# Zero matmuls on TensorE ahead of the transposes, the MLP loops and the router of a two-block transformer on one core

## The reference

```
# first block, two layers
x = x + rms(pool_mixer(rms(x)) )                      # layer 0 mixer
x = x + rms(relu(rms(x) @ w_up[0])**2 @ w_down[0])    # MLP, 4096 wide
k, v = split(rms(x) @ w_kv)
x = x + rms(stick_breaking_attention(rms(x) @ w_q, k, v) @ w_o)
x = x + rms(relu(rms(x) @ w_up[1])**2 @ w_down[1])    # MLP
# second block
proj = rms(x) @ w_in                                  # conv parts, q, k, v
h = x + concat(short_conv(proj), diff_attention(proj)) @ w_out
# hierarchical mixture: softmax over 4 groups, top 2 of 8 experts in the best group
comb = router(rms(h))                                 # 256 x 32 weights
out = h + sum_e comb[:, e] * (silu(rms(h) @ w_gate[e]) * (rms(h) @ w_up[e])) @ w_down[e]
```

## Time and profile before

| | before |
|---|---|
| median of 3 runs | 1189.21 us (1184.12, 1189.39, 1189.21) |
| the profiled execution's own time | 1188.13 us |
| its span, first to last instruction | 1186.2 us |
| PE busy | 957.2 us (81%), 5929 matmul records |
| PE weight loads | 715.6 us (60%) |
| DVE, ACT busy | 487.4 us (41%), 374.7 us (32%) |
| mean granted TensorE clock | 0.914 of full |
| DMA | 310.34 MB, mean 262 GB/s |

### The profile page before, as it was taken

One profiled execution on the slowest core, in us unless ns is written; L12 is line 12 of the kernel. 1 busy time (PEld: TensorE's weight loads), 2 busy tenths in 40 slices (PEclk: granted clock), 3 DMA queues, 4 the chain that ended last, 5 costly groups with the idle time before them and its releaser, 6 DMA issues.

```text
span 1186.2 us, 14708 instructions
## 1 busy us (share of the span) xinstructions
PE 957.2 (81%) x5929; PEld 715.6 (60%) x5929; DVE 487.4 (41%) x746; ACT 374.7 (32%) x633; POOL 1.9 (0%) x7
## 2 busy tenths in 40 slices
PE   5799999699778899999698887966666676666666
PEld 4799999599546899899588764431323142424232
DVE  3655655654545656556656674220202020201010
ACT  3545544554343545445454441100000000000000
POOL 0000000000000000000000000000000000000000
PEclk9899999899999899999899998996979787878889
DMA  9454554445103445545250477699999999999996
GB/s 361 185 212 155 199 212 150 150 145 211 71 1 142 151 152 212 192 161 212 72 179 35 181 292 307 281 431 429 429 433 430 430 431 431 433 431 431 429 427 248
DMA packets 62731, 310.34 MB, mean 262 GB/s; under 512 B 2529, under 2 KB 3553, under 8 KB 52321
## 3 DMA queue, kind: packets, MB, share of 16 engines
q1 hardware_dynamic: 62256, 308.17, 64.7%
q0 software_dynamic: 432, 1.57, 0.4%
HBM read 308.68 MB, written 1.05 MB: 261 GB/s over the span
## 4 chain that ended last, share of the span: by engine, by line
PE 64%; DMA 16%; DVE 12%; ACT 5%; issue 2%; SPq 1%; DVEq 0%; ACTq 0%
DMA ring<-in_w_exp_down 16%; PE ps L599 14%; PE ps L600 13%; PE ps L601 13%; PE ps L976 6%; PE ps L995 5%; PE ps L957 5%; PE ps L1007 2%; DVE w_lo L1392 2%; DVE hT_lo L1365 1%; SPq L558 1%; ACT h L1039 1%; PE ps L618 1%; ACT w_hi L1097 1%; PE ps L651 1%
## 5 line engine op out<-in xcount | busy, mean ns | idle before, releaser
L1378 DVE TENSOR_TENSOR w_lo<-ring,w_hi 128x1024 fp32r<-128x1024 f32 x162 | 195.2, 1223 | 114.1 <-ACT w_hi L1082 114.1
L599 PE MATMUL ps<-hT_hi,w_hi 128*128 128x256 f32 x736 | 213.1, 290 | 9.9 <-DVE hT_lo L1365 7.9
L600 PE MATMUL ps<-hT_lo,w_hi 128*128 128x256 f32 x736 | 210.8, 286 | 0.0
L601 PE MATMUL ps<-hT_hi,w_lo 128*128 128x256 f32 x736 | 210.6, 286 | 0.0
L976 PE MATMUL ps<-ring,x 128*32 128x512 f32 x992 | 133.4, 698 | 75.2 <-DMA ring<-in_w_exp_up 65.2
L1082 ACT ACTIVATE w_hi<-ring 128x1024 fp32r<-128x1024 f32 x162 | 168.9, 1053 | 73.3 <-PE ps L601 67.5
L599 PEld LDWEIGHTS ps<-hT_hi,w_hi 128*128 128x128 f32 x736 | 143.8, 195 | 12.8 <-issue 10.8
L600 PEld LDWEIGHTS ps<-hT_lo,w_hi 128*128 128x128 f32 x736 | 143.8, 195 | 0.8 <-issue 0.2
L601 PEld LDWEIGHTS ps<-hT_hi,w_lo 128*128 128x128 f32 x736 | 143.7, 195 | 0.0
L976 PEld LDWEIGHTS ps<-ring,x 128*32 128x32 f32 x992 | 40.3, 126 | 162.8 <-issue 162.8
L995 PE MATMUL ps<-ring,moe 128*32 128x512 f32 x512 | 70.6, 712 | 53.9 <-DMA ring<-in_w_exp_down 52.6
(11 more groups left out here) (241 smaller groups left out, 1058.8 us busy)
## 6 DMA issues: line engine op xcount, KB each, us to landing
ring<-in_w_exp_down SPq DMA_DIRECT2D x32, 2048.0 KB, 19.5
ring<-in_w_exp_gate SPq DMA_DIRECT2D x31, 2048.0 KB, 18.9
ring<-in_w_exp_up SPq DMA_DIRECT2D x31, 2048.0 KB, 21.8
ring<-in_w_up SPq DMA_DIRECT2D x16, 2048.0 KB, 7.8
ring<-in_w_down SPq DMA_DIRECT2D x16, 2048.0 KB, 7.6
ring<-in_w_in SPq DMA_DIRECT2D x6, 2048.0 KB, 8.1
ring<-in_w_kv SPq DMA_DIRECT2D x4, 2048.0 KB, 9.4
ring<-in_w_q SPq DMA_DIRECT2D x2, 2048.0 KB, 8.1
```

Source lines behind the costliest of these rows:

```text
L599: mm(out, a_hi, b_hi, start=start, stop=False, skip_group_check=True)
L600: mm(out, a_hi, b_lo, start=False, stop=False, skip_group_check=True)
L601: return mm(out, a_lo, b_hi, start=False, stop=stop, skip_group_check=True)
L1378: ve.tensor_tensor(w_lo[:, f, :].rearrange("p (k w) -> p k w", k=KD), src, w_hi[:, f, :].rearrange("p (k w) -> p k w", k=KD).bitcast(F32), ...
```

## The change

A helper `keep_busy(bank, count)` issues `count` matmuls of zeros, each 128x128 by 128x512, from `zero_t` into one PSUM bank. Nothing reads what they write: bank 7 and bank 1 are overwritten by what follows, and bank 0 holds zeros anyway where they are written into it. It is called at nine points of the executed program, with 149 matmuls in all: 14 ahead of the transposes of the first MLP, 11 behind the transposes of each MLP, 40 behind each MLP, 10 behind the attention's output projection, 4 behind the second block's output projection, 8 behind the transposes there, and 11 behind the router's place counts. The other engines' programs are the same.

```diff
+            def keep_busy(bank, count):
+
+                for _ in range(count):
+                    mm(ps[:, bank, :], zero_t[:, 0:P], zero_t[:, 0:COLS], start=True, stop=True)
+
...
                         mm(acc[:, s, half * COLS:(half + 1) * COLS], zero_t[:, 0:P], zero_t[:, 0:COLS],
                            start=True, stop=True)
+                if layer == 0:
+                    keep_busy(0, 14)
                 transposes(x, x_ready, x_count)
+                keep_busy(0, 11)
                 pe.wait_ge(hT_lo_ready, 4 * turn + 4)
...
             mlp(0, 0, 2)
 
 
+            keep_busy(7, 40)
             transposes(h, h_ready, 4)
...
                 project(m)
 
+            keep_busy(7, 10)
             pe.wait_ge(mg_ready, 4)
             pe.wait_ge(ss_ready, 12)
             mlp(1, 2, 6)
 
 
+            keep_busy(7, 40)
             transposes(h, h_ready, 6)
...
+            keep_busy(7, 4)
             transposes(x, x_ready, 10)
+            keep_busy(1, 8)
 
             for k in range(KD):
...
             mm(wk(1)[:, 128:160], ones, ind[:, 1, :], start=False, stop=True).then_inc(pos_done, 1)
+            keep_busy(7, 11)
```

## The result

| | before | after |
|---|---|---|
| median | 1189.3 us (4 runs, 1184.12 to 1189.53) | 1180.3 us (4 runs, 1179.04 to 1180.71) |
| ratio to before, 95% interval | | 0.9932 (0.9910 to 0.9953) |
| profiled execution's span | 1186.2 us | 1178.2 us |
| mean granted TensorE clock | 0.914 | 0.929 |
| PE busy, matmul records | 957.2 us, 5929 | 971.3 us, 6078 |

The predicted time was 1180.5 us. With 149 more matmuls PE is busy for 14 us longer, and the kernel is faster by 9 us, 0.7%. That is small, but the interval leaves 1 out, and it is more than the 0.5% that the prediction took for telling a change from none.

The account below looks back on a forecast made before the run. The experts' DMA stream was taken to set the end, its start moved by earlier savings: 3.6 + 2.8 + 1.7 + 0.4 = 8.5 us, less 0.8, leaves 7.7 off 1188.1, 1180.4 us; median put at 1180.5 us, range 1176 to 1189.

Parts of the forecast that it names:

- What bounds: Expert half limited by DMA with a stream of fixed length; time saved ahead of it moves the kernel's end as much.
- The trains' length: In PE's gaps: 40 zeros take 9.1 us of 9.89; every train fits with 0.3 to 0.8 us to spare.
- Zeros hold the clock: All trains: the unknown, bounded by no effect on the clock and 8.5 us of gain as with real matmuls; the latter taken.
- The slower rival: Zeros don't hold the clock, so trains overrun behind the MLPs and in the router: some 10 us slower, 1198 us; chance 0.11.
- The transposes: At the MLPs' edges, full clock saves 1.0 us each behind and 0.8 us each ahead, 3.6 us; router's transposes nothing.
- The 0.8 us taken off: Ahead of the second MLP, an unfilled wait of 1.6 us was taken to cost the clock: one edge's transposes deducted.
- The gather, the term that failed: Router's first gather, its first part at 0.50: 7.92 us against 7.54 in the next group, so 0.4 us saved.
- The term put at nothing: the projections behind the MLPs: The projections behind the MLPs already begin at full clock, so nothing is saved there.
- The half case: Clock still falls in what is left of the gaps: 4 us saved, 1184.5 us; chance 0.2. Includes gather delayed by 1.8 us.

Follow-up runs that it names:

- Experiment 5: The changed kernel with the trains behind the MLPs 60 long in place of 40: 1188.27 us, ratio 1.0003 to the kernel before.
- Experiment 7: The changed kernel with the trains of 40 multiplying real activations (hT_hi) in place of zeros: 1181.14 us, ratio 0.9936 to the kernel before.
- experiment 6: The changed kernel with the trains behind the MLPs 20 long in place of 40: 1185.45 us, ratio 0.9970 to the kernel before.
- experiment 2: The changed kernel with only the trains around the MLPs' openings kept (14 and 10 ahead, 11 behind the transposes): 1184.70 us, ratio 0.9966 to the kernel before.
- experiment 4: The changed kernel without the train of 4 and the last train of 11 ahead of the gather: 1180.77 us, ratio 0.9946 to the kernel before.
- experiment 9: The kernel of experiment 8 without the last train of 11: 1177.95 us, ratio 0.9905 to the kernel before.
- experiment 8: The changed kernel with DVE writing the router's h in the contiguous order the gather reads: 1175.88 us, ratio 0.9899 to the kernel before.
- experiment 10: The changed kernel with two more trains in the attention, 13 and 10 zeros: 1180.16 us, ratio 0.9930 to the kernel before.
- experiment 3: The changed kernel with only the 8 zeros behind the router's transposes kept: 1187.47 us, ratio 0.9997 to the kernel before.
- experiment 11: Experiment 8 plus attention trains, 4 zeros ahead of the second MLP, 7 before `ind`, last train 10, no train of 4: 1174.59 us, ratio 0.9878 to before.

## Why the prediction was right, point by point

**What bounds.** That time saved ahead of the first expert weights comes off the end held in every profile to within 2 us: from the first expert matmul to the end of the span it is 438.1 us before and 438.8 after, and 437.7 to 439.5 in the profiles of the experiments. DMA paces it, and its start is what moved.

**The trains' length.** 40 were to take 9.1 us and took 9.27 with the last one's duration; 14, 11 and 8 came as computed. Experiment 5 shows that the spare time was needed: 20 matmuls more cost what they take, less the slack.

**Zeros hold the clock.** This was the unknown with both bounds. Experiment 7 settles it: the same train with data gives the same durations and the same clock behind it, 1.00, and experiment 6 shows the clock falling where the train is too short. The slower rival falls with it; its price for an overrun, though, is what experiment 5 shows, and what experiment 6 shows at the last train. The assumption that zeros in another bank don't slow the reads of PSUM held too: ACT's `hT_hi` took 487 ns before and 488 after, DVE's `hT_lo` 476 ns in both (medians).

**The transposes.** 1.0 us each behind the MLPs and 0.7 ahead of them, against 1.0 and 0.8 forecast. The Trainium skill's rule (TensorE: Matmul & The Clock Gate, Part 4) that transpose-mode doesn't get the full clock would have left 3.5 of the 8 us out, if `nc.tensor.transpose` is what that section means, which the trace doesn't say. Sixteen transposes took 2.05 us at a granted 1.00, against 3.63 us at 0.50. The kernel before shows more. In the first MLP's opening PE did nothing but these transposes at 0.50, and in the wait behind them the clock stood at 1.00 (stretch, columns as in rows 3):

```profile
37.30:40.30 3.00, 0.00 (x0) 0.00 (x0) 3.00 (x8) 3.00 (x9) 0.00 (x0) 1.00 0.38 102
```

So transposes alone came before a rise of the clock. The prediction cited the earlier trace rows for a clock of 1.00 behind the transposes, but those rows have the MLP's first matmuls 0.21 us apart, at 0.50 again: the clock had risen and fallen once more around the wait of 3.35 us.

**The 0.8 us taken off.** In the profiled execution after, the wait of 1.39 us ahead of the second MLP did not cost the clock, so the sum without the deduction was the nearer one for that edge. In experiments 2, 4, 6, 7 and 9 it did (the sixteen took 3.3 to 3.6 us); in 5, 8 and 10 it did not. Where it did, the opening took 0.3 us longer, and 0.7 in experiment 7. So 0.8 us was the top of what it can cost, for something that goes one way or the other from execution to execution.

**The gather, the term that failed.** I forecast 0.4 us from the difference between 7.92 us in the first group and 7.54 in the next, and put it down to the clock. It was 0.04 us. The step that failed is that attribution. The 7.92 was read from the timeline and the 7.54 from the chain, which counts the second gather only from the end of its forerunner; in the timeline it takes 7.68 us. The other 0.2 us isn't the clock either: in the kernel after, whose first gather ran at 1.00, the two take 7.88 and 7.68. I hadn't looked at the weight loads, 338 ns each, with matmuls 0.24 us apart where the contiguous gather has 0.12. Experiment 8 shows the loads to be the pace, and experiment 9 that the clock matters once they aren't.

**The term put at nothing: the projections behind the MLPs.** The prediction had them begin at full clock already, as its profile shows. That holds for one execution. Four profiles have no full train there: before and experiments 2, 3 and 6. At four of their eight edges the projection began at half clock, with 15 to 22 matmuls 0.09 us further apart, 1.4 to 2.0 us each. Behind a train of 40 or 60, at twenty edges in ten profiles, it never did. So the trains of 40 are worth more on average than the 1.0 us each that the profiled pair shows.

**The number.** That 1180.5 met 1180.3 us is partly luck. The sites of the profiled pair gained 8.1 us and the medians 9.0, where 7.7 had been added up: 0.8 us had been taken off for a clock that stayed, 0.4 us of the gather never came, and the projections' share wasn't in the sum.

**The half case's side mechanism.** A clock that falls ahead of the last train, and a gather 1.8 us late, was priced in the prediction and is in the profiles of experiments 6 and 10 at that size. It didn't come in the execution profiled after. Since that train bought nothing there (experiment 4), it could only cost.

What stays open: why the same idle stretch of 1.4 to 1.9 us costs the clock in one execution and not in the next, and what makes the attention stage vary by 2 us and the second block by 4 us (128.4 to 132.2 without a train of its own) between profiles, beyond the projections' starts. That slow stretches come, go and move about in both is seen (the second block has one of them in experiment 8 and two in the kernel after); that they are the whole of it isn't.

## What to carry to other kernels

Look at the granted clock behind each wait of TensorE, and price what follows the wait at both clocks; only what is on the path and paced by columns gains. In this kernel a train of zeros had to nearly fill its gap and end ahead of the data (20 in a gap of 10 us lost the clock, 60 came late), and a gap left open just before it could make it run at half clock and overrun. So fill the wait that loses the clock and not only the one behind it. When an instruction doesn't speed up with the clock, look at its weight loads. Here the order of the words cost 3.9 us and hid the clock's share. And compare more than one profile of each kernel before a stage is put down as running at full clock.

## What the runs showed of the hardware that was not expected

- The gather's float32 weight load of 128x128 took 335 ns with every eighth word of a row and 192 ns with adjacent words, both at a clock of 1.00 (the kernel after, and experiment 11, whose gather stood at 1.00 throughout). At 0.50 it was 338 and 333 ns (before and experiment 9). The Trainium skill (TensorE: Matmul & The Clock Gate, Part 2) says of the load that "Timing scales with column count P". Both loads have 128 columns, so here the measurement says that the order of the words counts too. It doesn't say so for every instruction: the transposes take x and h with the same stride, and their loads took 192 ns at 1.00; which of their two operands is loaded the profile doesn't say.
- The strided side moved to DVE costs less: its two writes of h, reading every eighth word, took 1140 ns each against 745 before, off the path.
- Zeros and data gave the same clock and the same duration, 9.27 and 9.23 us for forty.
